# A tile's expert sum moved ahead of the next tile's dots, and VectorE's recurrence steps moved behind the conv taps of their slot

## The chip, the cores and the metric

The kernel runs on one core of a Trainium2 chip. The metric is the device time in microseconds (us) of one execution. Five engines work side by side, each through its own list of instructions in order: TensorE (PE in the profile), VectorE (DVE), ScalarE (ACT), GpSimd (POOL, which here issues the gathers) and SyncE (SP, which issues the other transfers). They wait for each other through semaphores.

## What is computed

One decoder layer on 1024 tokens of width 1024, in float32: a mixer of two branches (an RWKV-7 recurrence over 8 heads and a causal convolution with 31 taps), and then an expert layer in which every token picks 128 of 16384 experts. The expert layer is where most bytes move: for each token it reads 128 rows of 4 KB of a table u and 128 of a table v.

```python
S = (S * w_t[:, :, None, :] + sa[..., None] * (kk_t * a_t)[:, :, None, :]
     + v_t[..., None] * k_t[:, :, None, :])                  # the recurrence, step by step
...
h = h + (g_r * o_r + g_c * o_c) @ w_out[i]                   # the mixer
...
u = jnp.take(u_tab, ib, axis=0)                              # the experts, ib: 128 indices a token
coef = gb * jax.nn.gelu(jnp.einsum('cd,ced->ce', xb, u), approximate=False)
return jnp.einsum('ce,ced->cd', coef, jnp.take(v_tab, ib, axis=0))
...
ple_gate = jax.nn.sigmoid(rms_norm(h, ple_norm_g[i]) @ ple_w_gate[i])
h = h + ple_gate * (p[i] @ ple_w_proj[i])
```

## The kernel before

The 1024 tokens are 8 tiles of 128 (NT = 8). After a first phase (projections of the first 256 tokens, with the mixer of tile 0 woven in) the main loop runs over t = 0 to 10, and each t over 128 slots s. In round t the following pieces are interleaved, one slot at a time, and every engine's list is written out by hand in this order:

- the experts' u side of tile t: GpSimd gathers one u row per token and slot (`gather_u`, L761, five buffers), VectorE multiplies it with the normed tile c and adds up (`dot`, L1924, on `e_u` or `e_a_rstd`). c is made by `make_c` (L1818) at the head of the round;
- the experts' v side of tile t - 2 (LAG = 2): GpSimd gathers one v row per token and slot (`gather_v`, L778, six buffers), TensorE adds it, weighted, to `acc` (`add_tokens`, L1085); ScalarE lays out the weights (L1425, L1427). The first pieces of this for a new tile wait on ScalarE for the last add of the tile before (semaphore `s_vmm`);
- the mixer of tile t + 1 (`front`): preparation in slots 0 to 16, the recurrence in slots 20 to 64, the conv taps in slots 0 to 65, then the output products;
- the choice of experts of tile t (`head`, `select`: pieces of MAX, MAX_INDEX, MATCH_REPLACE on VectorE), and in rounds 0 and 1 projections of the later tokens (L1155, `behind_out`).

GpSimd's list is strictly one v gather, one u gather, slot by slot. A v gather of slot j waits until the add of slot j - 6 has released its buffer, a u gather until the dot of slot j - 5 has.

The recurrence handles two chunks of 64 tokens in a tile, each in 15 steps of TensorE with copies on ScalarE (L1213) and, after eight of them, sums and masks on VectorE: step 0 (L1553), 1 (L1555 to L1559), 5, 6 and 7 (L1562), 8 (L1565), 10 (L1568) and 14 (L1571, L1573). TensorE's next step mostly waits for them. `rec_step(s)` says which step belongs to slot s (two in three slots). TensorE and ScalarE issue it in slot s; VectorE issues its part in slot s + 1, that is after dot s + 1:

```python
r = rec_step(s - 1)
if r:
    rec(2 * n + r[0], r[1])
for a in taps_at(n, s):
    conv_tap(n, a)                 # L1659
```

When the last token of a tile has been added, `summed` on VectorE adds `acc` to the tile's h (L1933, three instructions, reading `acc`), and only then may TensorE start `acc` for the next tile. It waits for all 128 adds of the tile. In the kernel before it stands after dot 1 of the next round. At slot 66 TensorE sums the conv result over channels (`conv_mean`, L942), for which the last taps must be done.

Of the kernel before, what the change touches and what calls it, by code (L numbers as in the profile page):

```python
# [21 lines left out]
NT = T // P  # L22
# [52 lines left out]
def col(tile, i):  # L75

    return tile[:, ds(i, 1)]
# [68 lines left out]
LAG = 2  # L146
# [40 lines left out]
def rec_step(s):  # L187

    j = -(-2 * (s - REC_AT) // 3)
    return divmod(j, REC_PE - 1) if s >= REC_AT and j < REC_STEPS and REC_AT + 3 * j // 2 == s else None  # L190


def taps_at(t, s):

    n = TAPS * CONV_TILES
    if t == 0:
        a, slots = s - CONV_AT - 8, CONV_SLOTS - 8
        return range(n * a // slots, n * (a + 1) // slots) if 0 <= a < slots else range(0)
    n -= EARLY_TAPS
    return range(EARLY_TAPS + n * s // MIX_AT, EARLY_TAPS + n * (s + 1) // MIX_AT) if s < MIX_AT else range(0)  # L200
# [30 lines left out]
def outputs_until(m):  # L231

    return sum(kind(i) in ("z", "conv") for i in range(m))
# [75 lines left out]
def trunk(nc, io, dram):  # L309

    with ExitStack() as ctx:
# [1224 lines left out]
        def _(dve):  # L1536
# [106 lines left out]
            def conv_tap(n, a):  # L1643
                j, i = divmod(a, CONV_TILES)
                base = n * TAPS * CONV_TILES
                out = gbc[:, 2, i, :]
                if a == 0:
                    if n:
                        dve.wait_ge(s_wu, (2 * n - 1) * KT)
                    if n:  # L1650
                        dve.wait_ge(s_hc, 16 * n)
                    else:
                        dve.wait_ge(s_ao, outputs_until(COL_TILES))
                        dve.wait_ge(s_up, 16 * 3)
                if j == 0:
                    dve.tensor_scalar(out, hc[:, i, 0:P], col(cw, i), col(vec, COL["dw_b"] + i), ALU.mult, ALU.add).then_inc(s_tap, 1)
                else:
                    dve.wait_ge(s_tap, base + a - CONV_TILES + 1)
                    dve.scalar_tensor_tensor(out=out, in0=hc[:, i, j:j + P], scalar=col(cw, j * CONV_TILES + i), in1=out,  # L1659
                                             op0=ALU.mult, op1=ALU.add).then_inc(s_tap, 1)  # L1660
# [4 lines left out]
            def conv_centred(n):  # L1665
                dve.wait_ge(s_cs, 2 * n + 1)
                dve.tensor_scalar(cmean, pd[:, HALF:HALF + P], 1.0 / CONV_W, None, ALU.mult).then_inc(s_cv, 1)
                dve.wait_ge(s_cv, 5 * n + 1)
                dve.tensor_tensor(gbc[:, 2, :, :], gbc[:, 2, :, :], over_tiles(cmean), ALU.subtract).then_inc(s_cv, 1)

            def conv_variance(n):
                dve.wait_ge(s_cs, 2 * n + 2)
                dve.tensor_scalar(crstd, pd[:, HALF:HALF + P], 1.0 / CONV_W, LN_EPS, ALU.mult, ALU.add).then_inc(s_cv, 1)
                dve.wait_ge(s_cv, 5 * n + 3)
                dve.reciprocal(crstd, crstd).then_inc(s_cv, 1)

            def conv_normed(n):
                dve.wait_ge(s_ca, 6 * n + 2)
                dve.tensor_tensor(gbc[:, 2, :, :], gbc[:, 2, :, :], over_tiles(crstd), ALU.mult).then_inc(s_cv, 1)
# [69 lines left out]
            def y_centred(n):  # L1749
                dve.wait_ge(s_mean, n + 1)  # L1750
                flat = y[:, :, :].rearrange("p i t -> p (i t)")
                dve.scalar_tensor_tensor(out=flat, in0=pd[:, 0:HALF], scalar=-1.0 / HD, in1=flat, op0=ALU.mult,
                                         op1=ALU.add).then_inc(s_cen, 1)

            def y_variance(n):
                dve.wait_ge(s_yvar, n + 1)
                dve.tensor_scalar(yrstd, pd[:, 0:HALF], 1.0 / HD, GN_EPS, ALU.mult, ALU.add).then_inc(s_ys, 1)
                dve.wait_ge(s_ys, 9 * n + 1)
                dve.reciprocal(yrstd, yrstd).then_inc(s_yvinv, 1)
# [14 lines left out]
            def y_gated(n):  # L1774
                dve.wait_ge(s_ys, 9 * n + 9)
                dve.tensor_tensor(y[:, :, :], y[:, :, :], gbc[:, 0, :, :], ALU.mult).then_inc(s_y, 1)
# [150 lines left out]
            def summed(n):  # L1927
                dve.wait_ge(s_hhin, 16 * (n + 1))
                dve.wait_ge(s_vmm, (n + 1) * NSEL)
                for h in range(D // HALF):  # L1930
                    cols = slice(h * HALF, (h + 1) * HALF)
                    for rows, from_ in SUM_ROWS[h]:
                        dve.tensor_tensor(hh[rows, cols], hh[rows, cols], acc[from_, cols], ALU.add).then_inc(s_hh, 1)  # L1933
# [13 lines left out]
            def front(n, s):  # L1947
                if s in (0, 4, 5, 7, 10, 12, 14, 16):
                    prep(n, (0, 4, 5, 7, 10, 12, 14, 16).index(s))
                r = rec_step(s - 1)  # L1950
                if r:
                    rec(2 * n + r[0], r[1])
                for a in taps_at(n, s):
                    conv_tap(n, a)
                if s == MIX_AT + 1:
                    conv_centred(n)
                if s == MIX_AT + 2:
                    y_centred(n)
                if s == MIX_AT + 3:
                    conv_variance(n)  # L1960
                if s == MIX_AT + 4:
                    y_variance(n)
                if s == MIX_AT + 5:
                    conv_normed(n)
                if s == MIX_AT + 6:
                    y_scaled(n)
                if s == MIX_AT + 8:
                    y_bonus(n)
                    y_gated(n)
                if s == MIX_AT + 13:  # L1970
                    conv_gated(n)
                if s == MIX_AT + 23:
                    mix_gated(n)
                if s == MIX_AT + 24:
                    mix_summed(n)
                if n + 1 < NT:
                    for a in early_taps_at(n + 1, s):
                        conv_tap(n + 1, a)
                if s == MIX_AT + 32:
                    front_h(n, 0)  # L1980
                if s == MIX_AT + 35:
                    front_h(n, 1)
                    front_rstd(n)
                if NEXT_HEAD_AT <= s < NEXT_HEAD_AT + 8:
                    head(n, 0, s - NEXT_HEAD_AT)
                if NEXT_HEAD_AT + 8 <= s < NEXT_HEAD_AT + 14:
                    select(n, 0, s - NEXT_HEAD_AT - 8)
                if NEXT_HEAD_AT + 14 <= s < NEXT_HEAD_AT + 22:
                    head(n, 1, s - NEXT_HEAD_AT - 14)
# [33 lines left out]
            for s in range(FRONT_SLOTS, SLOTS):  # L2023
                front(0, s)
            for t in range(NT + LAG + 1):
                if t < NT:
                    make_c(t)
                for s in range(SLOTS):
                    if t < NT:
                        dot(t, s)  # L2030
                        if 0 <= s - head_slot(1) - 8 < 6:
                            select(t, 1, s - head_slot(1) - 8)
                        if s < head_slot(1) + 8:
                            head(t, 1, s - head_slot(1))
                    if s == (1 if t < NT + LAG else 0) and t > LAG:
                        summed(t - LAG - 1)
                    if s == 3 and 1 <= t <= NT:
                        coefficients(t - 1)
                    if t < NT:
                        for h in range(2, PH):  # L2040
                            if head_slot(h) <= s < head_slot(h) + 8:
                                head(t, h, s - head_slot(h))
                            if head_slot(h) + 8 <= s < head_slot(h) + 14:
                                select(t, h, s - head_slot(h) - 8)
                        if s == HEADS_END:
                            less_max(t)
                            indices_out(t)
                        if s == HEADS_END + 4:
                            softmax(t)
                            token_indices(t)  # L2050
                    if t < BLOCKS and s:
                        for m in behind_done(t, s - 1):
                            if kind(m) in ("z", "conv"):
                                behind_out(t, m)
                    if t + 1 < NT:
                        front(t + 1, s)
                    if tail_step(t, s):
                        tail(*tail_step(t, s))
# [71 lines left out]
```

## Time and profile before

| | us |
|---|---|
| median of 3 runs | 3707.6 (3706.2 to 3715.5) |
| the profiled execution | 3706.0 |
| its span | 3704.3 |
| TensorE busy | 2755.3 (74%) |
| VectorE busy | 2368.4 (64%) |
| GpSimd busy | 1979.5 (53%) |
| ScalarE busy | 525.3 (14%) |
| transfers | 1253.8 MB, mean 338 GB/s |

An engine's busy time is that of its recorded instructions; a row of waits says for how long an engine stood idle ahead of an instruction and what ended that ("remote" is a release that the profile can't name, "issue" time in which it waited for nothing that the profile shows). TensorE's ends are modelled. Rounds of the main loop begin, by `make_c`, at 277, 610, 946, 1346, 1742, 2127, 2523 and 2914 us; the rounds without dots follow from 3283 us on.

### The profile page before, as it was taken

The page shows a single profiled execution, that of the slowest core. Times are in us where ns is not written, and L with a number is a line of the kernel's source. Part 1 is how long each engine was busy: PE and PEld are TensorE (multiplying, and loading weights), DVE is VectorE, ACT ScalarE, POOL GpSimd, SP SyncE. Part 2 cuts the span into 40 slices and gives each one's busy share as a digit, 9 for nine tenths or more (in the row PEclk, how much of TensorE's full clock was granted, in tenths as well). Part 3 has the DMA queues.
Part 4 walks back from the last instruction along what each step waited for, and adds up shares of the span by engine and source line. Part 5 has one row for each costly group of instructions (what it writes and reads, how often), then busy time and mean ns, then how long its engine had stood idle before and what let it go on. Part 6 is the DMA issues. An engine that isn't in the chain of part 4 may idle for free.

```text
span 3704.3 us, 41438 instructions
## 1 busy us (share of the span) xinstructions
PE 2755.3 (74%) x15264; PEld 1272.2 (34%) x15264; DVE 2368.4 (64%) x6063; ACT 525.3 (14%) x1165; POOL 1979.5 (53%) x2093
## 2 busy tenths in 40 slices
PE   9988988998657766676567756775667777677877
PEld 7764655556233322332133213331333112111111
DVE  4549889888767677676867686768675665520000
ACT  3222112221101010111110011101110121110000
POOL 0003334334556666566656665666566666656663
PEclk9999999999767877787778867886788778779999
DMA  6538899889999999999999999999999999999995
GB/s 194 178 133 278 295 319 344 284 285 333 355 323 345 404 378 360 335 394 370 367 334 396 380 366 333 383 382 385 331 362 402 409 388 373 379 372 356 373 354 207
DMA packets 381194, 1253.76 MB, mean 338 GB/s; under 512 B 40384, under 2 KB 76480, under 8 KB 380224
## 3 DMA queue, kind: packets, MB, share of 16 engines
q0 software_dynamic: 294912, 1073.87, 77.6%
q1 hardware_dynamic: 83776, 176.20, 13.4%
q8 instruction: 120, 1.97, 0.2%
q10 hardware_dynamic: 2304, 1.05, 0.1%
q14 instruction: 82, 0.67, 0.0%
HBM read 1221.47 MB, written 29.49 MB: 338 GB/s over the span
## 4 chain that ended last, share of the span: by engine, by line
PE 19%; DVE 18%; another core or an unknown queue 15%; issue 11%; DMA 10%; POOL 8%; ACT 2%; SPq 0%; POOLq 0%; DVEq 0%; ACTq 0%
DVE e_u L1924 6%; PE e_acc L1085 6%; DMA e_v<-in_v_tab,e_idxT 5%; POOL e_v L778 4%; DMA e_u<-in_u_tab,e_idx 3%; PE e_pd L983 2%; PE e_acc L1155 2%; POOL e_u L761 2%; DVE e_gbc L1659 2%; PE e_pd L1001 2%; PE e_pd L803 2%; DVE e_a_rstd L1924 2%; PE e_pd L1054 2%; PE e_pd L908 1%
## 5 line engine op out<-in xcount | busy, mean ns | idle before, releaser
L1085 PE MATMUL e_acc<-e_v,e_wd 128*32 128x512 f32 x3636 | 1079.2, 762 | 397.8 <-DMA e_v<-in_v_tab,e_idxT 269.2
L761 POOL DMA_INDIRECT e_u<-in_u_tab,e_idx x820 | 797.2, 972 | 863.2 <-DVE e_dots L1924 412.8
L1924 DVE CUSTOM_DVE_ANT_0 e_u<-e_u,e_c 128x1024 f32<-128x1024 f32 x820 | 996.0, 1215 | 311.5 <-DMA e_u<-in_u_tab,e_idx 251.7
L778 POOL DMA_INDIRECT e_v<-in_v_tab,e_idxT x909 | 866.0, 953 | 613.2 <-issue 220.4
L1085 PEld LDWEIGHTS e_acc<-e_v,e_wd 128*32 128x32 f32 x3636 | 145.0, 120 | 976.4 <-DMA e_v<-in_v_tab,e_idxT 581.1
L1155 PE MATMUL e_acc<-e_v 128*128 128x384 f32 x1216 | 434.3, 501 | 24.7 <-DMA e_v<-in_w_in 16.6
L1659 DVE SCALAR_TENSOR_TENSOR e_gbc<-e_hc,e_cw,e_gbc 128x128 f32<-128x128 f32 x960 | 310.4, 344 | 1.9 <-issue 0.6
L1924 DVE CUSTOM_DVE_ANT_0 e_a_rstd<-e_a_rstd,e_c 128x1024 f32<-128x1024 f32 x204 | 247.8, 1215 | 73.4 <-DMA e_a_rstd<-in_u_tab,e_idx 63.1
L803 PE MATMUL e_pd<-e_arena 64*64 64x64 f32 x3584 | 168.8, 251 | 159.8 <-ACT e_arena L1213 70.8
L1155 PEld LDWEIGHTS e_acc<-e_v 128*128 128x128 f32 x1216 | 224.7, 193 | 178.2 <-issue 28.6
L761 POOL DMA_INDIRECT e_a_rstd<-in_u_tab,e_idx x204 | 198.3, 972 | 130.8 <-DVE e_dots L1924 87.7
L803 PEld LDWEIGHTS e_pd<-e_arena 64*64 64x64 f32 x3584 | 144.2, 160 | 306.6 <-issue 129.6
L1933 DVE TENSOR_TENSOR e_hh<-e_hh,e_acc 64x512 f32<-64x512 f32 (+1 forms) x24 | 16.4, 683 | 275.2 <-remote 139.5
L1213 ACT ACTIVATE e_arena<-e_pd 128x512 f32<-128x512 f32 (+1 forms) x192 | 90.4, 471 | 708.8 <-remote 345.4
L983 PE MATMUL e_pd<-e_w_out,e_actT 128*128 128x512 f32 x256 | 138.2, 671 | 35.4 <-DVE e_actT L1790 26.7
L1001 PE MATMUL e_pd<-e_actT,e_w_q 128*128 128x128 f32 x1024 | 143.6, 296 | 17.0 <-issue 8.7
L1001 PEld LDWEIGHTS e_pd<-e_actT,e_w_q 128*128 128x128 f32 x1024 | 133.0, 208 | 63.0 <-issue 48.4
L1129 PE MATMUL e_acc<-e_w_q,e_u 128*128 128x256 f32 x608 | 141.5, 386 | 3.4 <-DVE e_w_q L2008 3.4
L1085 PE MATMUL e_acc<-e_u,e_wd 128*32 128x512 f32 x368 | 121.7, 629 | 25.3 <-DMA e_u<-in_v_tab,e_idxT 16.2
L1054 PE MATMUL e_pd<-e_w_out,e_actT 128*128 128x512 f32 x256 | 125.8, 625 | 2.3 <-ACT e_actT L1261 2.3
L1129 PEld LDWEIGHTS e_acc<-e_w_q,e_u 128*128 128x128 f32 x608 | 114.5, 192 | 23.2 <-issue 5.2
L778 POOL DMA_INDIRECT e_u<-in_v_tab,e_idxT x92 | 86.7, 943 | 48.9 <-issue 23.7
(266 smaller groups left out, 2761.1 us busy)
## 6 DMA issues: line engine op xcount, KB each, us to landing
e_v<-in_w_in SPq DMA_DIRECT2D x76, 512.0 KB
e_u<-in_w_in SPq DMA_DIRECT2D x38, 512.0 KB, 3.7
e_v<-in_v_tab,e_idxT POOLq DMA_INDIRECT x909
e_u<-in_u_tab,e_idx POOLq DMA_INDIRECT x820
e_ring<-in_w_c SPq DMA_DIRECT2D x32, 256.0 KB
e_zb<-in_w_c SPq DMA_DIRECT2D x32, 256.0 KB
e_ring<-in_w_r SPq DMA_DIRECT2D x32, 256.0 KB
e_zb<-in_w_r SPq DMA_DIRECT2D x32, 256.0 KB
```

The lines of the kernel that those rows point to most:

```text
L761: pool.indirect_dma_start(out=u[m % UR][:, :], out_offset=None, in_=io["u_tab"], in_offset=bass.IndirectOffsetOnAxis(ap=idx[n % 2][:, j:j ...
L778: pool.indirect_dma_start(out=v[i], out_offset=None, in_=io["v_tab"], in_offset=bass.IndirectOffsetOnAxis(ap=idxT[n % (LAG + 1)][:, k:k + ...
L803: last = pe.matmul(pi[r, out, i * CH:(i + 1) * CH], a[r, i, :], b[r, i, :] if len(b.shape) == 3 else b[r, :], start=True, stop=True)
L983: last = pe.matmul(pd[:, h * HALF:(h + 1) * HALF], mixt[:, k, :], w_out[:, k, h * HALF:(h + 1) * HALF], start=(k == 0), stop=(k == KT - 1))
L1001: last = pe.matmul(pd[:, h * P:(h + 1) * P], w_q[:, k, h * P:(h + 1) * P], actT[:, k, :], start=(k == 0), stop=(k == KT - 1))
L1054: last = pe.matmul(pd[:, h * HALF:(h + 1) * HALF], actT[:, k, :], w_ple[:, k, h * HALF:(h + 1) * HALF], start=(k == 0), stop=(k == KT - 1))
L1085: last = pe.matmul(acc[rows, cols], w[:, at_:at_ + 32], v[v_place(m)[0]][:, cols], start=(step == 0), stop=True, skip_group_check=True)
L1129: last = pe.matmul(out, w_a[m % UW][:, k, :], ahead[:, k, :], start=(k == 0), stop=(k == KT - 1))
L1155: last = pe.matmul(acc[:, m % 2 * HALF:m % 2 * HALF + BEHIND_T], w_b[m % 2][:, k, :], behind[:, k, :], start=(k == 0), stop=(k == KT - 1))
L1213: act.activation(dst, src, ACT.Copy).then_inc(s_ra, 1)
L1659: dve.scalar_tensor_tensor(out=out, in0=hc[:, i, j:j + P], scalar=col(cw, j * CONV_TILES + i), in1=out, op0=ALU.mult, op1=ALU.add).then_in ...
L1924: dve.tensor_tensor_reduce(u[m % UR][:, :], u[m % UR][:, :], c[:, :], 1.0, 0.0, ALU.mult, ALU.add, dots[n % 2][:, j:j + 1]).then_inc(s_dot, 1)
```

## The change

Two pieces of VectorE's list move; no instruction is added or removed, on any engine.

1. In `front`, VectorE's part of a recurrence step is issued in the slot of TensorE's, behind that slot's conv taps, instead of in the next slot, behind the next dot and ahead of the next taps.
2. `summed` for the finished tile is issued at the head of the round, ahead of `make_c` and all dots.

```diff
             def front(n, s):
...
-                r = rec_step(s - 1)
+                for a in taps_at(n, s):
+                    conv_tap(n, a)
+                r = rec_step(s)
                 if r:
                     rec(2 * n + r[0], r[1])
-                for a in taps_at(n, s):
-                    conv_tap(n, a)
...
             for t in range(NT + LAG + 1):
+                if t > LAG:
+                    summed(t - LAG - 1)
                 if t < NT:
                     make_c(t)
...
-                    if s == (1 if t < NT + LAG else 0) and t > LAG:
-                        summed(t - LAG - 1)
```

The list of TensorE, ScalarE, GpSimd and SyncE is the same in both kernels. VectorE, from one dot of round 4 to the third recurrence step of that kind, before (L1562 steps 5, 6 and 7; L1924 the dots; L1659 conv taps; L1852 to L1866 pieces of the experts' choice):

```order
L1924 ISA e_u0,e_dots0<-e_u0,e_c 128x1024
L1924 ISA e_dots0 128x1
L1852 MAX_INDEX e_pos<-e_best,e_onehot 128x8
L1853 MATCH_REPLACE e_onehot<-e_best,e_onehot 128x256
L1562 TENSOR_TENSOR e_arena<-e_pd,e_arena 128x256
L1659 SCALAR_TENSOR_TENSOR e_gbc<-e_hc,e_cw,e_gbc 128x128 x2
L1924 ISA e_u1,e_dots0<-e_u1,e_c 128x1024
L1856 MAX e_best<-e_onehot 128x8
L1659 SCALAR_TENSOR_TENSOR e_gbc<-e_hc,e_cw,e_gbc 128x128
L1924 ISA e_u2,e_dots0<-e_u2,e_c 128x1024
L1859 MAX_INDEX e_pos<-e_best,e_onehot 128x8
L1562 TENSOR_TENSOR e_arena<-e_pd,e_arena 128x256
```

and with the change:

```order
L1659 SCALAR_TENSOR_TENSOR e_gbc<-e_hc,e_cw,e_gbc 128x128
L1562 TENSOR_TENSOR e_arena<-e_pd,e_arena 128x256
L1924 ISA e_u0,e_dots0<-e_u0,e_c 128x1024
L1924 ISA e_dots0 128x1
L1852 MAX_INDEX e_pos<-e_best,e_onehot 128x8
L1853 MATCH_REPLACE e_onehot<-e_best,e_onehot 128x256
L1659 SCALAR_TENSOR_TENSOR e_gbc<-e_hc,e_cw,e_gbc 128x128 x2
L1924 ISA e_u1,e_dots0<-e_u1,e_c 128x1024
L1856 MAX e_best<-e_onehot 128x8
L1659 SCALAR_TENSOR_TENSOR e_gbc<-e_hc,e_cw,e_gbc 128x128
L1562 TENSOR_TENSOR e_arena<-e_pd,e_arena 128x256
L1924 ISA e_u2,e_dots0<-e_u2,e_c 128x1024
```

Step 5 now stands ahead of the dot on `e_u0` and step 6 ahead of the dot on `e_u2`; two dots stand between them in both lists.

VectorE at the change from round 2 to round 3, before (L1818 is c, L1933 the finished tile's sum, L1597 the mixer's first preparation):

```order
L1849 MAX e_best<-e_onehot 128x8
L1818 SCALAR_TENSOR_TENSOR e_c<-e_x,e_stats,e_gt 128x1024
L1924 ISA e_a_rstd,e_dots1<-e_a_rstd,e_c 128x1024
L1852 MAX_INDEX e_pos<-e_best,e_onehot 128x8
L1853 MATCH_REPLACE e_onehot<-e_best,e_onehot 128x256
L1597 TENSOR_TENSOR e_actT<-e_arena,e_vec 128x512
L1659 SCALAR_TENSOR_TENSOR e_gbc<-e_hc,e_cw,e_gbc 128x128
L1924 ISA e_u0,e_dots1<-e_u0,e_c 128x1024
L1856 MAX e_best<-e_onehot 128x8
L1933 TENSOR_TENSOR e_hh<-e_hh,e_acc 128x512
L1933 TENSOR_TENSOR e_hh<-e_hh,e_acc 64x512 x2
```

and with the change:

```order
L1849 MAX e_best<-e_onehot 128x8
L1933 TENSOR_TENSOR e_hh<-e_hh,e_acc 128x512
L1933 TENSOR_TENSOR e_hh<-e_hh,e_acc 64x512 x2
L1818 SCALAR_TENSOR_TENSOR e_c<-e_x,e_stats,e_gt 128x1024
L1924 ISA e_a_rstd,e_dots1<-e_a_rstd,e_c 128x1024
L1852 MAX_INDEX e_pos<-e_best,e_onehot 128x8
```

The sum moves ahead of c, two dots and the preparation's first instruction.

## Rows read from the trace of the kernel before

**Rows 1.** stretches: tile 0's slots 20 to 66, and the three of tile 4

```profile
core 0: us, PE busy (x) PEld busy (x) DVE busy (x) ACT busy (x) POOL busy (x), PEclk, DMA share, GB/s
336.50:470.89 134.39, 127.01 (x1010) 79.47 (x1011) 106.90 (x299) 27.56 (x62) 44.91 (x47) 0.97 0.85 282
1742.99:1801.42 58.43, 38.44 (x137) 9.59 (x137) 56.01 (x139) 14.12 (x29) 39.06 (x39) 0.69 0.97 376
1801.42:1951.99 150.57, 91.44 (x919) 45.10 (x917) 100.30 (x280) 16.41 (x40) 89.07 (x95) 0.75 0.94 335
1951.99:2128.21 176.22, 132.02 (x573) 56.38 (x573) 128.56 (x319) 14.05 (x34) 114.79 (x121) 0.82 1.00 390
```

**Rows 2.** waits of VectorE, 946 to 2914 us: total, times, longest

```profile
DVE e_arena L1571 <- remote: 69.8, 8, 9.7
...
DVE e_arena L1562 <- PE e_pd L803: 44.4, 9, 6.0
```

**Rows 3.** waits of TensorE, the same stretch

```profile
PE e_acc L1085 <- DVE e_hh L1933: 46.6, 4, 15.0
...
PE e_pd L803 <- DVE e_arena L1562: 32.8, 14, 4.3
...
PE e_pd L942 <- DVE e_gbc L1659: 9.3, 4, 2.4
```

**Rows 4.** timeline of VectorE, tile 4: start, length, line, work, [idle before]

```profile
1834.98 0.42 DVE L1562 TENSOR_TENSOR e_arena<-e_pd,e_arena 128x256 f32<-128x256 f32 x1 [5.55 <-PE e_pd L803]
1835.33 0.60 DVE L1659 SCALAR_TENSOR_TENSOR e_gbc<-e_hc,e_cw,e_gbc 128x128 f32<-128x128 f32 x2
1835.85 1.21 DVE L1924 CUSTOM_DVE_ANT_0 e_u<-e_u,e_c 128x1024 f32<-128x1024 f32 x1
...
1839.13 0.40 DVE L1562 TENSOR_TENSOR e_arena<-e_pd,e_arena 128x256 f32<-128x256 f32 x1
```

**Rows 5.** timeline of TensorE, tile 0, the recurrence's second step

```profile
342.10 1.12 PE L825 MATMUL e_pd<-e_zb 64*64 64x64 f32 x16 [6.28 <-DVE e_arena L1553]
```

**Rows 6.** timeline of all engines at the change into tile 6

```profile
2513.80 1.05 PE L1085 MATMUL e_acc<-e_v,e_wd 128*32 128x512 f32 x4 [0.76 <-DMA e_v<-in_v_tab,e_idxT]
...
2522.69 1.29 DVE L1818 SCALAR_TENSOR_TENSOR e_c<-e_x,e_stats,e_gt 128x1024 f32<-128x1024 f32 x1 [2.34 <-issue]
...
2526.21 0.23 ACT L1425 ACTIVATE e_wd<-e_zero 128x16 f32<-128x16 f32 x1 [31.15 <-remote]
...
2527.59 1.21 DVE L1924 CUSTOM_DVE_ANT_0 e_a_rstd<-e_a_rstd,e_c 128x1024 f32<-128x1024 f32 x1
...
2529.07 2.10 DVE L1933 TENSOR_TENSOR e_hh<-e_hh,e_acc 128x512 f32<-128x512 f32 x3
...
2529.84 2.74 PE L1085 MATMUL e_acc<-e_v,e_wd 128*32 128x512 f32 x6 [14.99 <-DVE e_hh L1933]
```

**Rows 7.** timelines of ScalarE and VectorE at three other tile changes

```profile
1346.42 0.23 ACT L1425 ACTIVATE e_wd<-e_zero 128x16 f32<-128x16 f32 x1 [13.71 <-PE e_acc L1085]
...
1741.59 1.29 DVE L1818 SCALAR_TENSOR_TENSOR e_c<-e_x,e_stats,e_gt 128x1024 f32<-128x1024 f32 x1 [1.64 <-issue]
...
1743.65 0.23 ACT L1425 ACTIVATE e_wd<-e_zero 128x16 f32<-128x16 f32 x1 [30.07 <-remote]
...
2126.90 1.27 DVE L1818 SCALAR_TENSOR_TENSOR e_c<-e_x,e_stats,e_gt 128x1024 f32<-128x1024 f32 x1
...
2128.05 0.23 ACT L1425 ACTIVATE e_wd<-e_zero 128x16 f32<-128x16 f32 x1 [24.32 <-remote]
```

**Rows 8.** timeline of GpSimd, tiles 4, 6 and 7

```profile
1751.62 0.94 POOL L778 DMA_INDIRECT e_v<-in_v_tab,e_idxT  x1 [5.19 <-PE e_acc L1085]
...
2533.41 0.94 POOL L778 DMA_INDIRECT e_v<-in_v_tab,e_idxT  x1 [4.79 <-PE e_acc L1085]
2534.65 1.01 POOL L761 DMA_INDIRECT e_a_rstd<-in_u_tab,e_idx  x1 [0.30 <-DVE e_dots L1924]
...
2923.70 0.94 POOL L778 DMA_INDIRECT e_v<-in_v_tab,e_idxT  x1 [3.47 <-PE e_acc L1085]
```

## The prediction

> **What bounds the kernel now.** I read the stretches first, then the waits, then the timelines around the two places that the change touches. The stretches [rows 1] cut one tile of the main loop at its slots: 0 to 20 last 58.4 us, 20 to 66 (the recurrence's slots) 150.6 us, 66 to 128 last 176.2 us. The reader is to see three different limits. In the first VectorE is busy 56.0 of 58.4 us. In the last the DMA engines' share is 1.00 at 390 GB/s. In the middle nothing is full: VectorE 100 of 150.6 us, 335 GB/s, TensorE's records 91 us. There the engines wait for each other. The waits between 946 and 2914 us (tiles 2 to 6) say who: VectorE sits before its recurrence steps L1571 and L1562 until TensorE has delivered [rows 2], and TensorE waits for VectorE's L1562, though less [rows 3]. In tile 0 the same slots take 134.4 us with TensorE busy 127 us: it is the bound there, since no v is added.
>
> The profiled execution took 3706.0 us (span 3704.3 and 1.7 around it), the median of the runs is 3707.6; I add to 3706.0. About 0.3%, 11 us, is what a measurement of this kernel can tell from no change.
>
> **Part 1: recurrence steps one slot earlier.** No instruction is added. On VectorE one dot and the heads' piece of that slot now stand behind a step instead of ahead of it. What counts is what lies *between* two steps, and that stays the same in number: between one L1562 and the next there were two dots and there are two dots. [Rows 4] show such a pair: VectorE wakes at 1834.98 after 5.55 us of waiting for TensorE, works without a gap through two dots (the first at 1835.85) and reaches the next step at 1839.13. With the change VectorE wakes at the same moment, since it was waiting, and still has two dots to do. So this lateness, which looks like what the change removes, stays. I put the gain of every step behind a waiting one at 0 (bounds: above, the 32.8 us that TensorE waited for L1562, [rows 3]; below nothing, rival 5). The same rows give the unit: 4.15 us less the step (0.42), three taps (0.9) and halved is 1.4 us for a dot with its piece of a head.
>
> A gain remains where the *first* step of a tile is late. In tile 0 TensorE idled 6.28 us for L1553 [rows 5]; 1.4 us of what stood before it goes, and so in tile 1. In tiles 2 to 6 the first step waited for TensorE, so nothing. The price is at the stage's end. The last step (L1571, waited for up to 9.7 us, [rows 2]) resets VectorE to TensorE, and then one dot and a head's piece more stand before the last taps, for which TensorE already waits (9.3 us, 4 times, [rows 3]): 1.4 us later. In tiles 0 and 1 gain and price cancel: 0. In tiles 2 to 6 one u gather less is through when the DMA-bound stretch begins: 128 rows of 4 KB are 0.524 MB, at that stretch's 390 GB/s 1.3 us [rows 1], five times: **+6.5 us** (bounds 0, if the queue catches up unseen, and 5 x 1.4 = 7 us).
>
> **Part 2: the tile's sum ahead of c and the dots.** Five tile changes matter (into tiles 3 to 7); later ones have no dots. Into tile 6 [rows 6] TensorE's last add is recorded at 2513.80, VectorE makes c at 2522.69, sums at 2529.07, and TensorE resumes at 2529.84 after 14.99 us. The sum (three instructions, 2.1 us) now stands ahead of c. But it also waits for the *release* of the tile's last add, and that is not the recorded end: ScalarE's L1425 waits for the same add, and starts at 2526.21. VectorE was ready for c at 2522.69 - 2.34 = 2520.35, so it would now wait 5.9 us. In the same way [rows 7]: into tile 4 ready at 1741.59 - 1.64 = 1739.95, released 1743.65, a wait of 3.7 us; into tile 5 2126.90 against 2128.05, 1.2 us; into tile 3 it was released at 1346.42, 0.1 us after VectorE was ready; into tile 7 it came before c, and I put 0. Of these waits 1.6 and 2.3 us lie where VectorE idled anyway: 0.1 + 2.1 + 1.2 + 3.5 = 6.9 us are new, at the head of the one stretch in which VectorE is the bound. Behind the waiting sum stand c, every dot, and so every u gather. At slot 20 VectorE waits for TensorE again, so I charge half: **+3.5 us** (bounds 0 and 6.9).
>
> What it gives: the 5.6 us of c, two dots and prep between c and the sum (6.4 us less 0.8 of idling, [rows 6]) leave TensorE's stall, less the new waits: 5.6 + 3.5 + 4.4 + 2.1 + 5.6 = 21.2 us over the five. It reaches the end only through the gathers. GpSimd stood before a v gather for TensorE 5.19, 4.79 and 3.47 us (into tiles 4, 6 and 7, [rows 8]) and not into the other two. The u gather behind it needs dot 1, which had ended 5.8 us before that gather left (2527.59 + 1.21 against 2534.65, [rows 6, 8]) and now ends later by the sum and the new wait: 4.2, 5.6 and 2.1 us. So both leave 1.6, 0.2 and 3.5 us earlier: **-5.3 us** (bounds 0 and -21.2).
>
> **Sum:** 6.5 + 3.5 - 5.3 = +4.7 us, so 3706.0 + 5 = **3711 us**, no change that can be told; this case's own range is 3698 to 3722.
>
> **A rule against my sum.** The granted clock is 0.75 in the recurrence's slots of tile 4 and 0.97 in those of tile 0 [rows 1]: between the two levels 1.2 and 2.4 GHz in one, nearly always 2.4 in the other, with TensorE busy 91 of 151 us in one and 127 of 134 in the other. The Trainium skill, "TensorE: Matmul & The Clock Gate", Part 1 (the HAM clock gate), says that the throttled state is the default and that activity releases it; by that rule less idling on TensorE would buy a faster TensorE, and the trace agrees so far as these two rows go. By my sum the idling in these slots doesn't fall, so it adds nothing; where it falls, rival 2 has the price.
>
> **The rivals.**
> 1. *TensorE's stall at the tile change is on the path* (faster). For it: 46.6 us of waiting for L1933 [rows 3]. Against: behind it come 58 us in which VectorE is full. If all 21.2 us pass and nothing else costs: 3685. Chance 0.24.
> 2. *TensorE at 2.4 GHz in the recurrence's slots* (faster). They would shrink from 150.6 towards tile 0's 134.4 us; a third of that in five tiles is 27 us: 3679 (all of it, 81 us: 3625). Against: TensorE still waits there for copies and sums of others. Chance 0.06.
> 3. *The late steps do come earlier* (faster): half of 32.8 us is 16 us, 3690. It needs VectorE not to have waited at the step before. Chance 0.06.
> 4. *VectorE waits for the last add* (slower). The sum at the head of VectorE's tile holds c, dots and u gathers until the last add is released, up to 11.4 us after its recorded end (2513.80 + 1.05 against 2526.21, [rows 6]). If each of the five changes costs the worst case, 5.9 us, on the path: 3706 + 29 = 3735. It decides from the point where these waits pass the 5.3 us that the gathers gain. Chance 0.16.
> 5. *A step's wait now holds a dot* (slower). During each wait GpSimd stands before a u gather instead of a v gather, and goes on only after step, tap and dot (0.42 + 0.3 + 1.22 = 1.9 us, [rows 4]). If half a microsecond stays of each of four long waits in ten chunks, 20 us: with the rest of the sum 3731. Chance 0.10.
> That leaves 0.38 for the forecast. That the change doesn't do what it says is excluded: GpSimd, TensorE, ScalarE and SyncE keep their order, and VectorE's rows move as shown ahead.
>
> **How the numbers follow.** Faster by over 0.3%: rivals 1 to 3, 0.36. Slower: rivals 4 and 5, 0.26. Same: 0.38. The range, for 8 of 10, goes from a little below rival 1 (3680) to a little above rival 5 (3733); outside stay rival 2 and part of rival 4.
>
> **What would show it.** L1933 stands before L1818, with a wait of some us into tiles 4 and 6; TensorE's 46.6 us for L1933 fall to about 25; GpSimd's 5.19 and 4.79 us shrink. In the recurrence's slots VectorE's waits grow by about a dot each while the stretch stays near 150 us, and TensorE waits 1.4 us longer for the last taps. I am wrong if that stretch becomes shorter or longer by over 4 us, or if slots 0 to 20 change by over 3 us.

## The result, and the profile after

The changed kernel takes 3735.3 us (median of 6 runs), the kernel before 3711.2 us (6 runs in all): ratio **1.0057, 95% interval 1.0043 to 1.0072**, by the ratio some 21 us slower. On the 3706.0 us from which the prediction was summed, that is 3727 us. The profiled execution took 3735.8 us, its span is 3734.1 us.

The stretches of the kernel after, cut at the same slots as [rows 1]; first tile 0's slots 20 to 66, then the three of tile 4, then the slots 20 to 66 of tiles 2, 3, 5 and 6, last all of tiles 2 to 6, from slot 0 of tile 2 to slot 0 of tile 7 ("tile N" here means round N of the main loop):

```profile
core 0: us, PE busy (x) PEld busy (x) DVE busy (x) ACT busy (x) POOL busy (x), PEclk, DMA share, GB/s
337.05:471.80 134.75, 128.47 (x1014) 79.96 (x1015) 106.60 (x299) 27.78 (x62) 44.90 (x47) 0.99 0.84 279
1749.56:1809.80 60.24, 41.84 (x132) 11.28 (x129) 53.99 (x135) 10.74 (x23) 41.33 (x43) 0.65 1.02 398
1809.80:1966.82 157.02, 90.82 (x918) 44.42 (x916) 99.99 (x279) 16.41 (x40) 88.51 (x93) 0.75 0.89 321
1966.82:2155.10 188.28, 131.96 (x583) 54.48 (x584) 130.76 (x321) 17.39 (x39) 121.72 (x127) 0.81 0.99 379
...
1014.60:1169.90 155.30, 89.87 (x916) 43.90 (x914) 99.97 (x279) 16.31 (x40) 88.52 (x93) 0.79 0.89 321
1412.29:1569.21 156.92, 92.27 (x912) 45.22 (x912) 100.00 (x280) 15.93 (x39) 88.44 (x93) 0.75 0.89 318
2209.12:2364.52 155.40, 90.16 (x918) 44.27 (x916) 99.90 (x279) 16.30 (x40) 88.48 (x93) 0.79 0.90 324
2606.02:2759.52 153.50, 95.39 (x923) 47.28 (x920) 99.98 (x280) 16.41 (x40) 88.41 (x93) 0.77 0.91 328
...
952.76:2951.86 1999.10, 1323.41 (x8136) 552.37 (x8139) 1409.95 (x3621) 219.55 (x500) 1238.62 (x1285) 0.78 0.96 363
```

and of the kernel before, the same tiles 2 to 6 as a whole:

```profile
956.84:2915.62 1958.78, 1316.95 (x8126) 557.65 (x8126) 1411.44 (x3618) 218.88 (x500) 1234.77 (x1281) 0.77 0.98 368
```

Three things are to be seen. Tile 0 is unchanged (134.4 and 134.8 us). In tiles 2 to 6 the recurrence's slots grew, in tile 4 from 150.6 to 157.0 us, over the five tiles from 755.0 to 778.1 us, with every engine as busy as before; what fell is the DMA share, 0.94 to 0.89. And the last rows hold the account: 0.96 of 1999.1 us and 0.98 of 1958.8 us are nearly the same busy time. With two digits each product is good to 10 us only; summed from the trace's packets they are 1923 and 1913 us. **So of the 40 us that these tiles lose, 30 are time in which the DMA engines had no work, and 10 are more packets' time**: 725 MB moved for 721, gathers that fell behind these tiles before. The part behind them got 6.4 us shorter, and the stretch from slot 0 of tile 0 to slot 0 of tile 2 took 674.0 for 678.6 us, so that the span grew by 30 us in all.

The waits after, 945 to 2955 us, first VectorE's (total, times, longest):

```profile
DVE e_arena L1571 <- PE e_pd L889: 60.0, 6, 10.6
DVE e_arena L1562 <- remote: 49.7, 8, 9.7
DVE e_arena L1562 <- PE e_pd L803: 48.9, 6, 9.6
```

Of the kernel before, a second row of waits for L1562 (946 to 2914 us) belongs beside [rows 2]:

```profile
DVE e_arena L1562 <- remote: 31.5, 10, 7.2
```

TensorE's after:

```profile
PE e_pd L803 <- ACT e_arena L1213: 94.6, 30, 7.6
...
PE e_pd L803 <- DVE e_arena L1562: 25.3, 13, 4.1
PE e_pd L942 <- DVE e_gbc L1659: 13.8, 5, 2.9
PE e_acc L1085 <- DVE e_hh L1933: 11.8, 2, 9.7
```

GpSimd's waits after, 953 to 2952 us:

```profile
POOL e_u L761 <- DVE e_dots L1924: 163.2, 90, 5.5
...
POOL e_v L778 <- PE e_acc L1085: 95.9, 84, 2.6
```

and before, 957 to 2916 us:

```profile
POOL e_v L778 <- PE e_acc L1085: 145.1, 102, 5.2
...
POOL e_u L761 <- DVE e_dots L1924: 80.0, 72, 6.7
```

TensorE waits less for L1562 (25.3 for 32.8 us) and much less for the sum (11.8 for 46.6 us), VectorE's waits grew (for L1562 from 75.9 to 98.6 us in all, the longest from 7.2 to 9.7 us), and GpSimd's waiting for the dots on `e_u` doubled, 80 to 163 us: a dot is what it needs before it may issue a u gather.

One place shows how. VectorE and GpSimd in tile 3, at a chunk's step 8 (L1565), first before, then after; the last two rows after are stretches of 4 us:

```profile
1525.60 1.21 DVE L1924 CUSTOM_DVE_ANT_0 e_a_rstd<-e_a_rstd,e_c 128x1024 f32<-128x1024 f32 x1
...
1530.62 0.43 DVE L1565 TENSOR_TENSOR e_arena<-e_arena,e_m_id 128x256 f32<-128x256 f32 x1 [3.38 <-ACT e_arena L1213]
...
1530.29 0.94 POOL L778 DMA_INDIRECT e_v<-in_v_tab,e_idxT  x1 [1.67 <-PE e_acc L1085]
1532.72 0.94 POOL L761 DMA_INDIRECT e_u<-in_u_tab,e_idx  x1 [1.49 <-DVE e_dots L1924]
```

```profile
1536.46 0.42 DVE L1565 TENSOR_TENSOR e_arena<-e_arena,e_m_id 128x256 f32<-128x256 f32 x1 [4.44 <-ACT e_arena L1213]
1536.80 1.21 DVE L1924 CUSTOM_DVE_ANT_0 e_a_rstd<-e_a_rstd,e_c 128x1024 f32<-128x1024 f32 x1
...
1533.13 0.94 POOL L778 DMA_INDIRECT e_v<-in_v_tab,e_idxT  x1 [0.30 <-issue]
1538.29 0.94 POOL L761 DMA_INDIRECT e_a_rstd<-in_u_tab,e_idx  x1 [4.21 <-DVE e_dots L1924]
...
1532.00:1536.00 4.00, 3.01 (x8) 0.27 (x4) 0.01 (x1) 0.17 (x1) 1.77 (x2) 0.91 1.00 389
1536.00:1540.00 4.00, 3.52 (x60) 1.86 (x60) 3.54 (x10) 1.02 (x2) 1.41 (x2) 1.00 0.50 196
```

Before, the dot of that slot is done when VectorE starts to wait, and GpSimd, with that dot behind it, stands idle for 1.67 and 1.49 us. After, the dot stands behind the step: GpSimd has nothing to issue from 1534.07 to 1538.29, and the last row, a window of 4 us that the wait empties, shows the DMA engines at half (0.50, 196 GB/s). Before, no window of 4 us from 1492 to 1564 us is below 0.78.

The tile changes after, into tiles 4 to 7 (VectorE; each row covers the sum's three instructions, and c stands behind one of them):

```profile
1746.08 2.12 DVE L1933 TENSOR_TENSOR e_hh<-e_hh,e_acc 128x512 f32<-128x512 f32 x3
...
2151.62 2.12 DVE L1933 TENSOR_TENSOR e_hh<-e_hh,e_acc 128x512 f32<-128x512 f32 x3 [0.35 <-remote]
2153.78 1.29 DVE L1818 SCALAR_TENSOR_TENSOR e_c<-e_x,e_stats,e_gt 128x1024 f32<-128x1024 f32 x1
...
2548.52 2.12 DVE L1933 TENSOR_TENSOR e_hh<-e_hh,e_acc 128x512 f32<-128x512 f32 x3 [3.12 <-remote]
...
2948.38 2.12 DVE L1933 TENSOR_TENSOR e_hh<-e_hh,e_acc 128x512 f32<-128x512 f32 x3 [4.23 <-remote]
```

The sum stands ahead of c and waits for the last add three times, 7.7 us together, 4.2 us at most. The following slots 0 to 20 got shorter: tiles 5, 6 and 7 take 54.0, 54.0 and 51.3 us, before 64.5, 58.8 and 59.5.

### The profile page after: what moved, and what is told of

It reads as the page before. It is cut to its first block, busy times and chain, and to the rows that moved or that the text cites. A ratio compares the mean times of both kernels' runs of the same rounds, so it can differ in the third digit from the quotient of the medians.

```text
span 3734.1 us, 41438 instructions
## 1 busy us (share of the span) xinstructions
PE 2759.4 (74%) x15264; PEld 1268.9 (34%) x15264; DVE 2364.8 (63%) x6063; ACT 525.9 (14%) x1165; POOL 1980.9 (53%) x2093
## 3 DMA queue, kind: packets, MB, share of 16 engines
q1 hardware_dynamic: 83776, 176.20, 13.4%
## 4 chain that ended last, share of the span: by engine, by line
PE 21%; DVE 18%; DMA 12%; another core or an unknown queue 12%; issue 11%; POOL 8%; ACT 2%; SPq 0%; POOLq 0%; ACTq 0%; DVEq 0%
PE e_acc L1085 8%; DVE e_u L1924 6%; DMA e_v<-in_v_tab,e_idxT 6%; POOL e_v L778 4%; PE e_pd L983 2%; DMA e_u<-in_u_tab,e_idx 2%; PE e_acc L1155 2%; POOL e_u L761 2%; DVE e_gbc L1659 2%; PE e_pd L1054 2%; DVE e_a_rstd L1924 2%; PE e_pd L803 2%; PE e_pd L1001 2%; PE e_pd L908 1%
## 5 line engine op out<-in xcount | busy, mean ns | idle before, releaser
L1924 DVE CUSTOM_DVE_ANT_0 e_u<-e_u,e_c 128x1024 f32<-128x1024 f32 x820 | 994.7, 1213 | 307.9 <-DMA e_u<-in_u_tab,e_idx 230.5
L1659 DVE SCALAR_TENSOR_TENSOR e_gbc<-e_hc,e_cw,e_gbc 128x128 f32<-128x128 f32 x960 | 308.7, 342 | 2.9 <-issue 1.3
L1924 DVE CUSTOM_DVE_ANT_0 e_a_rstd<-e_a_rstd,e_c 128x1024 f32<-128x1024 f32 x204 | 247.5, 1213 | 77.5 <-DMA e_a_rstd<-in_u_tab,e_idx 63.5
L1933 DVE TENSOR_TENSOR e_hh<-e_hh,e_acc 64x512 f32<-64x512 f32 (+1 forms) x24 | 16.5, 686 | 279.6 <-PE e_acc L1085 269.5
L983 PE MATMUL e_pd<-e_w_out,e_actT 128*128 128x512 f32 x256 | 137.3, 667 | 34.1 <-DVE e_actT L1790 28.5
```

The costliest lines, as they stand in the source:

```text
L983: last = pe.matmul(pd[:, h * HALF:(h + 1) * HALF], mixt[:, k, :], w_out[:, k, h * HALF:(h + 1) * HALF], start=(k == 0), stop=(k == KT - 1))
L1924: dve.tensor_tensor_reduce(u[m % UR][:, :], u[m % UR][:, :], c[:, :], 1.0, 0.0, ALU.mult, ALU.add, dots[n % 2][:, j:j + 1]).then_inc(s_dot, 1)
```

## The experiments

Times are medians; each ratio is against the runs of the kernel before in the same set, that is, taken along with the run. Theory H says that a step's wait now holds a dot and the gathers behind it; in its sharper form, theory D, what counts is how long the DMA engines have no work in slots 20 to 66 of tiles 2 to 6. The rivals: S, that the loss comes from the wait for the last add at the tile change; and B, that GpSimd's issuing without a pause holds TensorE's deliveries.

**Each part alone.** Steps alone:

```diff
-                r = rec_step(s - 1)
-                if r:
-                    rec(2 * n + r[0], r[1])
                 for a in taps_at(n, s):
                     conv_tap(n, a)
+                r = rec_step(s)
+                if r:
+                    rec(2 * n + r[0], r[1])
```

> Only the recurrence steps move (behind the taps of their own slot); the sum stays in slot 1. Theory H (a step's wait now holds a dot, and behind the dot a u gather and the v gathers of GpSimd): nearly the whole loss is here, about +20 us against the kernel before; slots 20 to 66 of tiles 2 to 6 stay at 153 to 157 us each (149 to 153 before), GpSimd's waiting for dots in them at 25 us or more a tile. Theory S (the loss comes from VectorE's waits for the last add of a tile): within 4 us of the kernel before, and those slots return to 149 to 153 us.

Measured: 3733.3 us against 3710.0, ratio 1.0064 (1.0044 to 1.0083). The whole loss is here. Its stretch over tiles 2 to 6, and GpSimd's waits in it:

```profile
956.57:2953.09 1996.52, 1301.81 (x8126) 545.55 (x8126) 1408.11 (x3618) 217.52 (x496) 1239.64 (x1282) 0.78 0.96 362
...
POOL e_u L761 <- DVE e_dots L1924: 158.2, 85, 8.3
```

The sum alone:

```diff
             for t in range(NT + LAG + 1):
+                if t > LAG:
+                    summed(t - LAG - 1)
                 if t < NT:
                     make_c(t)
...
-                    if s == (1 if t < NT + LAG else 0) and t > LAG:
-                        summed(t - LAG - 1)
```

> Only the sum moves (ahead of c); the steps stay one slot later. Theory H: between -5 and +4 us against the kernel before, with the waits for the last add paid back in slots 0 to 20 by v gathers that leave earlier. Theory S: +15 to +21 us, the waits at the head of the tiles 3 to 7 as long as in the changed kernel or longer.

Measured: 3706.3 us, ratio 0.9986 (0.9970 to 1.0002). Theory S falls. VectorE's waits and TensorE's there:

```profile
DVE e_hh L1933 <- remote: 23.4, 5, 6.9
...
PE e_acc L1085 <- DVE e_hh L1933: 27.5, 3, 11.9
```

All five changes wait, 23.4 us together, against 46.6 us that TensorE waited before. Slots 66 to 128 of tiles 2 to 6 (to which the waiting sum now belongs) grow by 30.8 us, slots 0 to 20 of tiles 3 to 7 shrink by 34.1 us, to 54.0 us in four of them: what VectorE loses at the sum comes back behind it. The two parts multiply to 1.0050, within the interval of the whole.

**The other way, and where the sum stands.**

```diff
-                r = rec_step(s - 1)
+                r = rec_step(s - 2)
```

> The other way: the steps stand one slot later than in the kernel before, so one more dot is done ahead of each wait. Theory H, if its price is not only paid but also regained: VectorE's waiting before L1562 and L1571 falls in tiles 2 to 6 and their slots 20 to 66 get shorter by up to 4 us each, 5 to 20 us faster in all; tiles 0 and 1, where TensorE is the bound, lose 1 to 3 us each because TensorE waits for the steps. If the steps' lateness is what costs (the reason for which they would be moved forward): 10 to 25 us slower.

Measured: 3713.5 us, ratio 1.0011 (1.0001 to 1.0022): the expectation of a gain missed. Tiles 0 and 1 took 683.8 us, longer than the 673.6 to 678.6 us of the four kernels that have the same program up to there: the loss expected for them came, and larger. The slots 20 to 66 did get 13.4 us shorter, by what H said, yet the tiles 2 to 6 took 1962.8 us, not less than before:

```profile
965.33:2928.11 1962.78, 1301.96 (x8126) 547.73 (x8126) 1413.72 (x3618) 216.73 (x496) 1237.54 (x1283) 0.78 0.98 368
...
POOL e_u L761 <- DVE e_dots L1924: 54.5, 50, 5.9
POOL e_v L778 <- PE e_acc L1085: 159.3, 113, 5.2
```

GpSimd waits less for dots (54.5 for 80.0 us) and more for TensorE (159.3 for 145.1 us); the DMA share stays 0.98. By theory D, shorter slots with as much DMA work left over only hand it to slots 66 to 128, and these grew by 10.8 us. This run turned H into D, so D was made to fit it and isn't tested by it.

```diff
                 if t < NT:
                     make_c(t)
+                if t > LAG:
+                    summed(t - LAG - 1)
                 for s in range(SLOTS):
```

with the line in slot 1 removed, the steps as before.

> The sum stands behind c and ahead of dot 0, the steps as before. If the held c costs something of itself (ScalarE and the gathers don't need it, only the dots do), this is 1 to 3 us faster than the sum ahead of c; if only the wait for the last add matters, the two are the same within 1 us each way, since dot 0 stands behind the sum in both. Theory S: +15 us or more here too; theory H: within 4 us of the kernel before.

Measured: 3700.2 us, ratio 0.9974 (0.9957 to 0.9992): faster than the kernel before. The gain, some 10 us, is more than the 4 us that were expected at most. Its interval overlaps that of the sum ahead of c, so what c's place is worth isn't settled.

**Which crossing costs, and GpSimd's bursts.** The step in its own slot, but ahead of that slot's taps. Against the kernel before it is moved ahead of the next dot, as in the run with the steps alone, and of its own slot's taps too:

```diff
-                r = rec_step(s - 1)
+                r = rec_step(s)
```

> The steps stand in their own slot ahead of its taps: compared with the kernel before they pass the next slot's dot and piece of a head, but the taps of the slot now stand behind them. If the price is paid for the dot that stands behind the wait (theory H), nearly the whole loss of the run with the steps alone (+23 us, ratio 1.0064) is here too, +15 us or more. If it is paid because the step is late behind the taps of its slot (0.3 to 0.9 us of work), this one is clearly better than that run, +10 us or less.

Measured: 3739.9 us, ratio 1.0089 (1.0065 to 1.0114). To be ahead of the taps as well is no better (1.0089 against 1.0064, in different sets and with overlapping intervals), so the harm lies in what both runs share: the step moved ahead of the next dot and the piece of a head behind it. No run moves it past one of these two alone; it is the dot for which GpSimd waits.

Rests for GpSimd, after whose issues TensorE's late releases often came by 1 to 2.3 us in these traces (six small memsets that wait for each other, in every third slot; what declares them is left out here):

```diff
                     if t < NT:
                         gather_u(t, j)
+                    if LAG <= t < NT and REC_AT <= j < MIX_AT and j % 3 == 0:
+                        for i in range(6):
+                            pool.wait_ge(s_wz, rests)
+                            pool.memset(rest[:, :], 0.0).then_inc(s_wz, 1)
+                            rests += 1
```

> The kernel before; GpSimd rests in every third of the slots 20 to 65 of the tiles with both gathers: six small memsets that wait for each other, an estimate of 1.0 to 1.5 us, 15 times a tile (memset of 128x16: 0.11 us in the trace). It is busy 88 of 150 us there. Theory B (TensorE's releases are held while GpSimd issues without a pause: in the traces they come 1 to 2.3 us after the end of its last issue): the held releases get fewer, slots 20 to 66 shorter by 2 us a tile or more, 10 us or more faster. If the holding only coincides with the bursts, the rests cost nothing or up to 10 us.

> The run with the steps alone, with the same rests. There GpSimd's runs of issues without a pause are 4.4 long on average in these slots, against 3.2 before. Theory B: the rests give back 12 us or more of the 23 us. Theory H (held dots and the gathers behind them): the rests come on top, the loss stays at 20 us or grows to 35.

Measured: on the kernel before 3708.7 us, 1.0003 (0.9988 to 1.0017); on the steps alone 3747.4 us, 1.0111 (1.0088 to 1.0133), over the 1.0064 without them. The rests heal nothing, and theory B falls: it asked for 10 us or more faster. On the steps alone they seem to come on top, and the loss, some 41 us, is more than the 35 expected at most; but the run without them belongs to another set, and the run with the steps over the dot, in the same set, has 1.0089 (1.0065 to 1.0114), so what the rests add isn't settled.

**The first tiles alone.** `rec_step(s)` behind the taps for `n <= LAG`, `rec_step(s - 1)` ahead of them for the others.

> The steps are moved forward only in tiles 0 and 1 (the fronts of tiles 1 and 2), where no v is added and TensorE is the bound; from tile 2 on they stand as in the kernel before. Prediction of the step: gain and price cancel, 0, within 3 us each way. If the first steps' lateness (TensorE waited 12.1 us for L1553 there) was worth more than the later last taps: 3 to 6 us faster.

Measured: 3703.6 us, ratio 0.9992 (0.9977 to 1.0007): within 3 us of nothing, as forecast.

**In a faster set.** The next three ran in a set in which the kernel before takes 3484.4 us, 6% less than in all others. The record gives the same chip number (10) for this set and for the last one, taken 7 minutes later, in which it takes 3707.2 us again; what differs between them isn't known.

```diff
-UR, UW, VR, RING, RINGS = 5, 4, 6, 4, 8
+UR, UW, VR, RING, RINGS = 4, 4, 6, 4, 8
```

> The kernel before with four u buffers in place of five: no step moves, but at every wait of VectorE one u gather less (and the v gather behind it) can be under way. Theory D (the DMA engines are the bound of tiles 2 to 6 as a whole, and what counts is how long they run dry in slots 20 to 66; a held dot is one gather pair less under way): their idle time in these slots, 51 us over the five tiles before and 79 us with the steps alone, grows to 75 us or more, and the kernel is 20 us or more slower. If the order of VectorE's steps itself did the harm (TensorE's deliveries later because of it): within 5 us, apart from tiles 0 and 1.

```diff
+                r = rec_step(s - 2)
+                if r and r[1] == 14:
+                    rec(2 * n + r[0], r[1])
                 r = rec_step(s - 1)
-                if r:
+                if r and r[1] != 14:
                     rec(2 * n + r[0], r[1])
```

> Only the last step of each chunk (L1571, the longest waits: 88.7 us in 10 in tiles 2 to 6) stands one slot later, so one dot more is done ahead of it; the other steps as before. Theory D: the DMA engines' idle time in slots 20 to 66 falls by 5 to 10 us (10 waits, 0.5 to 1 us each), 3 to 10 us faster. If TensorE's wait for L1571 (14.7 us in 5 in those tiles) grows by a dot each time, it gives all of it back: within 3 us.

```diff
-                    if t >= LAG:
-                        gather_v(t - LAG, j)
+                    m = (t - LAG) * NSEL + j + 1
+                    if m == 1:
+                        gather_v(0, 0)
+                    if 1 <= m < NT * NSEL:
+                        gather_v(*divmod(m, NSEL))
```

> The kernel before, but GpSimd issues each v gather one slot earlier than the u gather of its slot, so that a u gather that stands before a held dot has one v gather more under way behind it, at the cost of waiting for TensorE's adds one slot earlier. Theory D: where the dots hold GpSimd (50 us in slots 20 to 66 of tiles 2 to 6) it gains, where TensorE holds it (163 us) it loses, as its lead over TensorE is six buffers either way; the idle time of the DMA engines changes by less than 10 us and may grow. From -8 to +15 us.

Measured: four u buffers 3513.0 us, 1.0087 (1.0074 to 1.0100); the last step later 3487.4, 1.0010 (1.0001 to 1.0019); v one slot ahead 3511.4, 1.0078 (1.0066 to 1.0091). The last step later gains nothing, where 3 to 10 us were expected if D held, and v one slot ahead, 27 us slower, lies outside its expected -8 to +15. Four u buffers lose 30 us, the size that D asked for, and still don't speak for it: in this set the DMA share of slots 20 to 66 is above 1 (below; packets overlap), so that by this measure there is no idle time that could grow. Of the four buffers' loss against the last-step run, 10.2 us lie in tiles 0 and 1 (683.6 for 673.4 us), 7.5 in tiles 2 to 6, 5.3 behind them. Of the loss of v one slot ahead against the same run, 16.2 of 25.8 us lie in tiles 2 to 6; why isn't known. That a smaller number of gathers under way empties the DMA engines in the slower sets was not tried.

**The two harmless pieces together.** The sum between c and dot 0, and the steps forward in tiles 0 and 1 only.

> The two pieces that did no harm, together: the sum between c and dot 0, and the steps forward in tiles 0 and 1 only. If the two runs apart add up (0.9974 and 0.9992), 0.9966, 10 to 15 us faster than the kernel before. Theory D: the idle time of the DMA engines in slots 20 to 66 of tiles 2 to 6 stays as in the kernel before, 48 to 58 us. If the sum's gain was chance: within 5 us of the kernel before.

Measured: 3696.1 us against 3707.2, ratio **0.9972 (0.9961 to 0.9983)**, 10 us faster than the kernel before and, ratio against ratio, some 31 us faster than the change. The forecasts of the time and of the idle time (51 us, below) both came.

**The account over all traces of the sets in which the kernel before takes some 3708 us.** Idle is (1 - DMA share) times length, summed over the five stretches of slots 20 to 66 (the share has two digits, so each is good to 4 us):

| kernel | tiles 2 to 6, us | slots 20 to 66, us | DMA idle in them, us |
|---|---|---|---|
| before | 1958.8 | 755.0 | 50 |
| sum alone | 1965.3 | 756.7 | 50 |
| steps later | 1962.8 | 741.6 | 51 |
| sum after c | 1959.1 | 755.4 | 53 |
| before, with rests | 1962.3 | 755.8 | 54 |
| steps forward in tiles 0, 1 | 1964.6 | 755.8 | 59 |
| both harmless pieces | 1956.2 | 754.2 | 51 |
| the change | 1999.1 | 778.1 | 81 |
| steps alone | 1996.5 | 779.3 | 80 |
| steps alone, with rests | 1998.7 | 790.8 | 85 |
| steps over the dot | 2001.9 | 787.1 | 93 |

The kernels fall into two groups, by the last column and by the first: 50 to 59 us idle and 1956 to 1965 us, 80 to 93 us idle and 1997 to 2002 us. The length of slots 20 to 66 doesn't sort them: the steps later have the shortest and no gain. That is what theory D says; it is first on record after all of these traces but that of both harmless pieces, so only that one's idle time was forecast by it. Against the kernel before, the idle time accounts for 31 of 40 us in the change, 30 of 38 with the steps alone, 43 of 43 with the steps over the dot; the table shows it going together with the held dot. No run emptied the DMA engines in another way in these sets, so the step from idle time to lost time is an account, not a separate test.

## Why the prediction was right and wrong, point by point

The sign was not the forecast's. It said no change that can be told, 3711 us; the measured ratio says 21 us slower, a case to which it gave 0.26. The measured time is inside the range by the ratio (3727), and the median of the changed kernel's own runs lies 2 us above it. That is luck in part: the sum was 16 us short, and the range holds the result only because its upper end was set by rival 5, which had the mechanism but a chance of 0.10.

- **What bounds the kernel.** "In the middle nothing is full: there the engines wait for each other" was read from the right row and concluded too early. A DMA share of 0.94 beside 1.00 and 0.97 in the other stretches says, by theory D, that over tiles 2 to 6 the DMA engines are the bound, 0.98 of 1959 us, and that the 50 us of idling in the middle are the only slack. I priced waits of TensorE and VectorE there, and not what they do to GpSimd's issues.
- **Part 1, the step that failed:** "What counts is what lies *between* two steps". The two dots between two steps did stay, and so did the lateness: TensorE's wait for L1562 went from 32.8 to 25.3 us, not by half. But what lies *ahead of the wait* changed: one dot less is done when VectorE stops, so GpSimd may issue one u gather less, and the v gather behind it. The term was +6.5 us (bounds 0 and 7); alone, this part costs 3710 x 0.0064 = 24 us. Its bound was too narrow as well, since it counted one gather a tile and not one at each long wait.
- **Rival 5** named this mechanism, with "half a microsecond of each of four long waits in ten chunks, 20 us" (3731, chance 0.10). Steps alone came to 24 us. Its condition, that the loss of a wait *stays*, was the question, and by theory D it stays because nothing else is slack. A reader of [rows 1] could have asked of each stretch how much of the DMA engines' time it leaves unused, and given this rival the chance of the forecast.
- **Tiles 0 and 1:** gain and price cancel. Right (0.9992), as was that tile 0 stays at 134 us.
- **Last taps 1.4 us later:** TensorE's wait for L1659 grew from 9.3 us in 4 to 13.8 in 5, 0.9 us for each of the five tiles where I had 1.4.
- **Part 2:** +3.5 - 5.3 = -1.8 us; alone it measured -0.14% = -5 us (-11 to +1). The waits for the last add came (23.4 us in five where I had 10.9; with both parts 7.7 in three), TensorE's wait for the sum shrank (46.6 to 27.5 us, with both parts to 11.8), and GpSimd's long waits for TensorE at the tile change shrank with it (5.2 to 2.6 us at most). Right in mechanism, and the size lies within the interval, which is wide. (One of the five terms under "What it gives" is 0.1 us too high, 5.6 for 5.5; it moves nothing.) **Rival 4** had its mechanism too, and its price didn't follow: slots 0 to 20 gave back 34.1 us for it. Of the 21 us of **rival 1** some 5 came with the sum ahead of c, and 10 with the sum behind it.
- **What would show it:** my two bounds for being wrong were both passed. Slots 20 to 66 grew by 2.2, 5.1, 6.4, 4.9 and 4.5 us, where 4 was the limit, and slots 0 to 20 changed by up to 10.4 us where I allowed 3.
- **The clock.** TensorE's granted clock in slots 20 to 66 of tiles 2 to 6 is 0.71 to 0.76 before and 0.75 to 0.79 after, between its levels 1.2 and 2.4 GHz each time, with the same 90 to 96 us of busy time in longer slots. The idling rose and the clock didn't fall. The Trainium skill's rule ("TensorE: Matmul & The Clock Gate", Part 1), that activity is what releases the throttled state, finds no support in these two traces. In the faster set, where TensorE is busy 85 to 88 of 117 to 120 us, the granted clock of these slots is 0.84 to 0.90, which goes the rule's way. What a faster clock would be worth here no run separates.

## What to carry to other kernels

Where one engine's steps are placed among work that lets another engine issue transfers, put that work ahead of the step that waits, not behind it: the place costs nothing in instructions, and a wait then runs over transfers that are already under way. Here one dot behind the wait cost 24 us, and one more dot ahead of it gained nothing. Before pricing a wait, add up each stretch's unused time of the resource that is full elsewhere (here 1 minus the DMA share, times the length): in this case a change was worth about what it did to that sum, and a stretch that got shorter with the same sum gained nothing. A sum that both frees an accumulator and waits for its last add can go to the head of a round when the work behind it catches up by itself.

## What the runs showed of the hardware that I had not expected

TensorE's releases come long after the recorded matmul, in slots with both kinds of gathers. In the run with the steps alone, TensorE's records and ScalarE's copy of the same result:

```profile
2304.29 1.15 PE L803 MATMUL e_pd<-e_arena 64*64 64x64 f32 x32
...
2313.58 0.60 ACT L1213 ACTIVATE e_arena<-e_pd 128x512 f32<-128x512 f32 x1 [8.36 <-remote]
...
2347.76 0.22 PE L872 MATMUL e_pd<-e_state,e_zb 128*64 128x64 f32 x1 [1.80 <-issue]
2348.49 0.22 PE L872 MATMUL e_pd<-e_state,e_zb 128*64 128x64 f32 x1 [0.51 <-issue]
```

The copy starts 8.1 us after the last of the 32 matmuls ends in the records, and at other places single matmuls come 0.7 us apart with nothing that they wait for. It is for such results that VectorE waits before L1562 and L1571. Counted from the trace's semaphore events, 117 releases of TensorE came over 3 us after the last recorded end of a matmul that gives them, in slots 20 to 66 of tiles 2 to 6 of this run, and none in tiles 0 and 1, where there are u gathers alone. In the kernel before they are 116 and in the change 108, so such late releases are not what the change added. Of the 116, 85 came 1 to 2 us after the end of GpSimd's last issue, and 28% of these stretches' time lies that far behind one; the rests brought the count in the run with the steps from 117 to 80 and didn't shorten the kernel. What makes them is open.

They are also absent in the faster set. The slots 20 to 66 of tile 4 there, in the run with the last step later:

```profile
1722.59:1842.70 120.11, 85.80 (x937) 40.78 (x936) 102.31 (x279) 15.70 (x38) 87.99 (x93) 0.90 1.02 405
```

120 us for 151, the DMA share at 1.02 and 405 GB/s, the granted clock 0.90, and no wait for L1562 or L1571 among VectorE's. None of TensorE's releases in slots 20 to 66 comes over 1 us late in this trace. So the same chip number can show the late releases in one set and not in the next, and the kernel before takes 3484 or 3708 us. That the late releases are what makes the slower sets slower is likely, but was not tested. Whether the change costs anything in the faster set was not measured; by theory D it would cost less, since no long wait empties the DMA engines there.
